# Layer 1's output projection in plain float32 from the weight ring, and seven expert homes taken over at the query products

## The reference

```python
h = rms_norm(x, l1_norm_attn)
x = x + mla_mixer(h, ...)            # ends in: out.reshape(B, S, 1024) @ w_out
h = rms_norm(x, l1_norm_ffn)
logits = h @ w_router                # top 2 of 8 experts, softmax of the two
for e in range(8):
    y = y + combine[..., e:e+1] * swiglu(h, w_gu[e], w_down[e])   # 1024 -> 2 x 3584 -> 1024
x = x + y
```

## Time and profile before

| | us |
|---|---|
| median of 3 runs | 1250.08 |
| lowest and highest run | 1250.06, 1251.47 |
| span of the profiled execution | 1247.9 |
| PE busy | 1208.8 (97%) |
| DVE busy | 530.3 (42%) |
| ACT busy | 336.5 (27%) |
| HBM read | 411.02 MB |

### The profile page before, as it was taken

How to read it: one execution, slowest core, us unless ns; L and a number is a source line. 1 busy time by engine, 2 the same in 40 slices (tenths; PEclk the granted TensorE clock), 3 DMA queues, 4 the chain that set the end, 5 groups by cost and what they waited for, 6 DMA issues and landing times.

```text
span 1247.9 us, 22143 instructions
## 1 busy us (share of the span) xinstructions
PE 1208.8 (97%) x9410; PEld 594.7 (48%) x9410; DVE 530.3 (42%) x1085; ACT 336.5 (27%) x654; POOL 64.0 (5%) x87
## 2 busy tenths in 40 slices
PE   9988999999988999999999999999999999999987
PEld 7767888888777733333433333333333333333321
DVE  6977665555777411331331143243232141413313
ACT  7365555454766300110220011011010012001101
POOL 5300000000530000000000000000000000000000
PEclk9999999999999999999999999999999999999999
DMA  9503545454605999999999999999999999999995
GB/s 345 196 19 138 195 176 187 182 196 121 231 6 223 385 383 418 397 380 417 423 420 423 423 421 422 423 422 406 423 423 421 423 422 421 423 423 420 422 423 233
DMA packets 61001, 413.58 MB, mean 331 GB/s; under 512 B 7120, under 2 KB 7280, under 8 KB 12640
## 3 DMA queue, kind: packets, MB, share of 16 engines
q1 hardware_dynamic: 60048, 411.20, 81.2%
q0 software_dynamic: 560, 0.81, 0.5%
q10 hardware_dynamic: 288, 0.08, 0.0%
HBM read 411.02 MB, written 1.05 MB: 330 GB/s over the span
## 4 chain that ended last, share of the span: by engine, by line
PE 82%; DVE 5%; SPq 4%; DMA 3%; ACT 3%; issue 1%; POOL 1%; DVEq 0%; ACTq 0%; POOLq 0%
PE PS L2465 37%; PE PS L2475 18%; PE PS L1936 6%; PE PS L1938 6%; PE PS L1937 6%; SPq L586 4%; DMA homes<-in_expert_tiles 2%; PE PS L2342 2%; DMA ring<-in_dense_tiles 1%; DVE w_lo L1243 1%; PE PS L2004 1%; PE PS L2049 1%; ACT arena L839 1%; PE PS L2374 1%; PE PS L1957 1%
## 5 line engine op out<-in xcount | busy, mean ns | idle before, releaser
L2465 PE MATMUL PS<-homes,arena 128*32 128x512 f32 x3736 | 409.7, 592 | 3.3 <-DMA homes<-in_expert_tiles 3.3
L2465 PEld LDWEIGHTS PS<-homes,arena 128*32 128x32 f32 x3736 | 120.1, 110 | 282.4 <-issue 270.5
L2475 PE MATMUL PS<-homes,arena 128*32 128x512 f32 x1928 | 213.5, 593 | 4.4 <-DMA homes<-in_expert_tiles 4.4
L1823 DVE SCALAR_TENSOR_TENSOR arena<-arena,PS 64x256 f32<-64x256 f32 x126 | 52.2, 414 | 379.2 <-ACT arena L1179 377.2
L1179 ACT ACTIVATE arena<-PS 64x512 f32<-64x512 f32 x63 | 37.3, 592 | 462.7 <-PE PS L2465 462.7
L1936 PE MATMUL PS<-w_hi,hT_hi 128*128 128x512 f32 (+2 forms) x372 | 141.8, 381 | 5.1 <-DVE w_lo L1243 3.0
L1938 PE MATMUL PS<-w_hi,hT_lo 128*128 128x512 f32 (+2 forms) x372 | 139.3, 374 | 0.0
L1937 PE MATMUL PS<-w_lo,hT_hi 128*128 128x512 f32 (+2 forms) x372 | 139.2, 374 | 0.0
L2475 PEld LDWEIGHTS PS<-homes,arena 128*32 128x32 f32 x1928 | 61.5, 110 | 149.8 <-issue 138.0
L2465 PE MATMUL PS<-arena 128*32 128x512 f32 x928 | 103.2, 592 | 2.2 <-DVE arena L1830 1.7
L1243 DVE TENSOR_TENSOR w_lo<-ring,w_hi 128x1024 fp32r<-128x1024 f32 (+1 forms) x60 | 66.9, 1160 | 32.8 <-ACT w_hi L784 32.6
(11 more groups left out here) (241 smaller groups left out, 1008.3 us busy)
## 6 DMA issues: line engine op xcount, KB each, us to landing
homes<-in_expert_tiles SPq DMA_DIRECT2D x270, 1024.0 KB, 20.2
arena<-in_expert_tiles SPq DMA_DIRECT2D x54, 1024.0 KB, 22.0
ring<-in_dense_tiles SPq DMA_DIRECT2D x49, 1024.0 KB, 4.8
arena<-in_expert_tiles SPq DMA_DIRECT2D x8, 512.0 KB, 7.3
arena<-in_expert_tiles SPq DMA_DIRECT2D x16, 256.0 KB, 7.5
x_res<-in_expert_tiles SPq DMA_DIRECT2D x4, 1024.0 KB, 10.3
ring<-in_dense_tiles SPq DMA_DIRECT2D x6, 512.0 KB, 6.2
ring<-in_dense_tiles SPq DMA_DIRECT2D x2, 832.0 KB, 4.3
```

Source lines behind the costliest of these rows:

```text
L1823: ins = v.scalar_tensor_tensor(out=act_exp[64 * j:64 * (j + 1), g, :], in0=gate[0:64, g, c], scalar=1.0, in1=PS[0:64, gu_banks[k][g], c], ...
L2465: ins = pe.matmul(PS[GROUP * q:GROUP * (q + 1), gu_banks[k][g], :], xT[:, cc, o + g * GROUP:o + (g + 1) * GROUP], quarter(k_home, q), star ...
L2475: ins = pe.matmul(PS[GROUP * q:GROUP * (q + 1), 3 + g, :], tokens_T(k, c, q // 2, g), quarter(k_home, q), start=k == 0 and c == 0, stop=end)
```

## The change

`NSPLIT` is the number of pieces that are still split: all but the four of `OUT1`. Those are multiplied as plain float32, with the ring place as the right operand and a new float32 tile `mT` (8 chunks by 256 tokens) as the left, one matmul in the program for each chunk. `mT` lies in home 12, where `hT_hi` is. In place of the split of the merged halves, DVE copies three of them from PSUM into `mT` and ACT the fourth. The splits of `OUT1` pieces are gone on both engines, inside attention and behind it. A ring place that held an `OUT1` piece is free for an expert piece once the piece is used, where it was free once it was split. The slots of `w_hi` and `w_lo` and home 13 are free once the last query piece that needs them is used. `HOME_OF` follows this: home 14, two ring places, the six slots, home 13, the two early homes, the three late ones, four ring places, home 12, the residual's. The early homes move from positions 8 and 9 of the round to 10 and 11.

```diff
--- before.py
+++ after.py
@@ -222,6 +222,8 @@
 LO_AHEAD = (5, 6)
 U0 = len(STREAM)
 
+NSPLIT = U0 - len(OUT1)
+
 
 
 
@@ -230,15 +232,15 @@
 SLAB_HOMES = 15
 RING_FIRST = 2
 HOME_OF = [14] + [(U0 - RING + i) % RING for i in range(RING_FIRST)]
+for _i in range(SLOTS):
+    HOME_OF += [RING + (NSPLIT - SLOTS + _i) % SLOTS, RING + SLOTS + (NSPLIT - SLOTS + _i) % SLOTS]
+HOME_OF.append(13)
+
+EARLY_HOME = SLAB_HOMES + LATE_HOMES
+HOME_OF += range(EARLY_HOME, EARLY_HOME + len(EARLY))
 HOME_OF += range(SLAB_HOMES, SLAB_HOMES + LATE_HOMES)
 HOME_OF += [(U0 - RING + i) % RING for i in range(RING_FIRST, RING)]
-for _i in range(SLOTS):
-    HOME_OF += [RING + (U0 - SLOTS + _i) % SLOTS, RING + SLOTS + (U0 - SLOTS + _i) % SLOTS]
-HOME_OF += [12, 13]
-
-EARLY_HOME = SLAB_HOMES + LATE_HOMES
-for _i in range(len(EARLY)):
-    HOME_OF.insert(1 + RING_FIRST + LATE_HOMES + 2 + _i, EARLY_HOME + _i)
+HOME_OF.append(12)
 RESIDUAL_HOME = EARLY_HOME + len(EARLY)
 HOME_OF.append(RESIDUAL_HOME)
 assert len(HOME_OF) == PLACES and len(set(HOME_OF)) == PLACES
@@ -353,6 +355,7 @@
         h = sb("h_tok", [P, NT, D])
         hT_hi = placed("hT_hi", [P, KC, SEQ], f32r, 12)
         hT_lo = placed("hT_lo", [P, KC, SEQ], f32r, 13)
+        mT = placed("mT", [P, KC, SEQ], f32, 12)
         aT_hi = placed("aT_hi", [P, 4, SEQ], f32r, 14)
         aT_lo = placed("aT_lo", [P, 4, SEQ], f32r, 14.5)
         ident = sb("ident", [P, P])
@@ -591,6 +594,9 @@
                 n = piece_floats(piece)
                 load(u, A["dense_tiles"][u, :, 0:n], n)
 
+            def last_in_ring(k):
+                return U0 - 1 - (U0 - 1 - k) % RING
+
             def first_free(m):
 
                 k = HOME_OF[m]
@@ -603,10 +609,14 @@
                     sp.wait_ge(pv_done, 32)
                 elif k >= SLAB_HOMES:
                     sp.wait_ge(scored, 16)
+                elif k < RING and last_in_ring(k) < NSPLIT:
+                    sp.wait_ge(lo_ready, 2 * (last_in_ring(k) + 1))
                 elif k < RING:
-                    sp.wait_ge(lo_ready, 2 * (U0 - (U0 - 1 - k) % RING))
+                    sp.wait_ge(used, last_in_ring(k) + 1)
                 elif k < RING + 2 * SLOTS:
-                    sp.wait_ge(used, U0 - (U0 - 1 - (k - RING)) % SLOTS)
+                    sp.wait_ge(used, NSPLIT - (NSPLIT - 1 - (k - RING)) % SLOTS)
+                elif k == 13:
+                    sp.wait_ge(used, NSPLIT)
                 else:
                     sp.wait_ge(used, U0)
 
@@ -789,7 +799,7 @@
             def split_ahead(u):
 
                 v = u + SLOTS
-                if v < U0:
+                if v < NSPLIT:
                     split_piece(v, piece_floats(STREAM[v]))
 
             def after(u, task=None):
@@ -870,12 +880,15 @@
                         exps(j + 2)
                     if j in HI_AHEAD:
                         split_ahead(ahead[HI_AHEAD.index(j)])
-                    if j == 4:
+                    if j == 4 and kind == "AB":
                         split_half(i0, 0, 0, 5)
-                    if j == 5:
+                    if j == 5 and kind == "AB":
                         split_half(i0 + 1, 0, 1, 1)
-                split_half(i0 + 2, 1, 0, 4)
-                split_half(i0 + 3, 1, 1, 5)
+                if kind == "AB":
+                    split_half(i0 + 2, 1, 0, 4)
+                    split_half(i0 + 3, 1, 1, 5)
+                else:
+                    split_bank(i0 + 3, mT[:, 4:8, P:2 * P], bank(5).rearrange("p (c n) -> p c n", c=4))
 
 
             a.dma_start(ident[:, :], A["ident"]).then_inc(ident_loaded, 16)
@@ -1081,9 +1094,6 @@
             transposed_heads(1, 1, range(4))
 
             attention(16, "C", [first(UQ) + i for i in range(len(UQ))], X_MERGE1)
-            for i in range(len(OUT1) - 2):
-                after(first(OUT1) + i)
-
             for g in range(2):
                 a.wait_ge(transposed, X_NORM3 + 2 * g + 1)
                 a.activation(x_cols[:, 4 * g:4 * g + 4, 0:P], bank(g).rearrange("p (c n) -> p c n", c=4), ACT.Copy)\
@@ -1252,7 +1262,7 @@
 
             def split_ahead(u):
                 w = u + SLOTS
-                if w < U0:
+                if w < NSPLIT:
                     split_piece(w, piece_floats(STREAM[w]))
 
             def after(u, task=None):
@@ -1304,7 +1314,14 @@
                 link(v.tensor_scalar(q_scale[:, 0, t, c0:c0 + nh], s, scale, None, ALU.mult))
                 link(v.tensor_scalar(q_scale[:, 1, t, c0:c0 + nh], s, -scale, None, ALU.mult))
 
+            def merged_half(i, t, g, b):
+
+                v.wait_ge(transposed, i + 1)
+                v.tensor_copy(mT[:, 4 * g:4 * g + 4, t * P:(t + 1) * P], bank(b).rearrange("p (c n) -> p c n", c=4))\
+                    .then_inc(lo_split, 1)
+
             def attention(s0, kind, ahead, i0):
+                half_done = split_half if kind == "AB" else merged_half
 
                 def front(i):
 
@@ -1397,17 +1414,18 @@
                     if j + 2 < 8:
                         front(j + 2)
                     if j == 5:
-                        split_half(i0, 0, 0, 5)
+                        half_done(i0, 0, 0, 5)
                     if j == 6:
-                        split_half(i0 + 1, 0, 1, 1)
+                        half_done(i0 + 1, 0, 1, 1)
                     if j in LO_AHEAD:
                         split_ahead(ahead[LO_AHEAD.index(j)])
                     if j % 4 == (2 if kind == "C" else 3):
                         final(j // 4, 0)
                     if j % 4 == 3:
                         final(j // 4, 1)
-                split_half(i0 + 2, 1, 0, 4)
-                split_half(i0 + 3, 1, 1, 5)
+                half_done(i0 + 2, 1, 0, 4)
+                if kind == "AB":
+                    split_half(i0 + 3, 1, 1, 5)
                 split_ahead(ahead[2])
 
             def add_residual(t, n, b):
@@ -1974,6 +1992,13 @@
             def chunk_products(u, t, out, k0, k1):
 
                 c0, w = STREAM[u][2], STREAM[u][4]
+                if u >= NSPLIT:
+                    pe.wait_ge(ring_loaded[u % RING], 16 * (u // RING + 1))
+                    for c in range(k0, k1):
+                        o = (c - c0) * w
+                        ins = pe.matmul(out, mT[:, c, t * P:(t + 1) * P], ring[:, u % RING, o:o + w],
+                                        start=c == 0, stop=c == KC - 1)
+                    return ins
                 s = u % SLOTS
                 for c in range(k0, k1):
                     o = (c - c0) * w
@@ -2134,7 +2159,10 @@
 
                 u0 = first(pieces)
                 for i in range(2):
-                    pe.wait_ge(lo_split, i0 + 3 + i)
+                    if pieces is OUT1 and i == 1:
+                        pe.wait_ge(hi_split, i0 + 1)
+                    else:
+                        pe.wait_ge(lo_split, i0 + 3 + i)
                     piece_products(u0 + i, 1, bank(6)).then_inc(used, 1)
                 piece_products(u0 + 2, 0, bank(1))
                 piece_products(u0 + 2, 1, bank(7)).then_inc(used, 1)
```

## The result

The changed kernel takes 1252.26 us in the median of 20 runs, against 1249.76 for the kernel before in as many. The ratio of the two is 1.0019, with an interval from 1.0013 to 1.0025: it is 2.4 us slower, between 1.6 and 3.1. The forecast was 1253.8, +3.7 on its own base.

A forecast was written before the change was run, and what follows sets the result against it. Weight transfers, waiting for homes that TensorE frees near 850 us, were taken to set the end. Products +5.8, attention -2.1 and homes 0 gave +3.7: span 1251.6, plus 2.2, is 1253.8 us (range 1249.6 to 1257.0).

The forecast's parts named there:

- The products: Output products behind attention: 30 plain float32 products at 0.88 us instead of 0.687, +5.8 us, bounds +5.3 to +7.1.
- the surplus of 0.009: Records of 192 columns take 0.171 us, 0.009 over the scaled 0.162; taken to give 0.441 at 512 columns.
- rival 4: Output products' weight loads: 0.11 us not hidden in each of 60 records, +6.6, 1260.4 us; chance 0.05.
- What leaves attention: Layer 1's attention: without output splits on ACT and DVE, the 22 products start at 396.6, not 398.71: -2.1 us.
- Homes earlier: Expert weight fills: seven more homes filled as the query products end, claimed to gain and cost nothing, 0 us.
- The end follows: Expert transfers wait for homes near 850 us, so the end moves with TensorE's first expert product, +3.7 us.
- Rival 1: Expert transfers: amount loaded sets the end, so earlier homes take 17.4 us off transfers; -5.5, 1244.6 us; chance 0.08.
- rival 2: End of the kernel: TensorE's 9.2 us of waits swallow its 3.7 us delay, 1250.1 us; chance 0.12.
- rival 3: Attention: another wait replaces the splits, so nothing is gained there; +5.8, 1255.9 us; chance 0.07.
- The sum: Whole kernel: span 1247.9 + 3.7 = 1251.6, plus 2.2 from span to median, 1253.8 us, +0.30%.
- the gain of 2.9: Attention: a gain of 2.9 with a product of 0.864 would put the time under 1252.6 us; chance 0.08.
- DVE's later mark: DVE's wait before marking the later slots ends 3.4 us later, covered because its next work comes 6.19 us after.

The follow-up runs named there:

- product-only kernel: Kernel before with only the 32 output products made plain float32; all splits and the fill order stay, ring places held until used: 1257.33 us, ratio 1.0061.
- hold_attention: Changed kernel with its seven early fills held back to the end of layer 1's attention: 1252.31 us, ratio 1.0024.
- ring_held: Kernel before with one SyncE edit: ring places that held an output piece are refilled after its products, not after its split: 1253.08 us, ratio 1.0025.
- old_order: Changed kernel with the order of homes of the kernel before put back: 1255.48 us, ratio 1.0050.
- hold_products: Changed kernel with the split slots' fills, and all 18 fills in the queue, held until the last output product: 1276.15 us, ratio 1.0211.
- half_products: Changed kernel with half of the output products left out (chunks 2 to 5 of the contraction): 1239.17 us, ratio 0.9917.
- attention_alone: Kernel before without the splits of the four output pieces, ring places held until their products: 1250.66 us, ratio 1.0003.

## Why the prediction was right

**The products, +5.8 said, +5.12 measured.** The step stands, and its size was off by 0.7 us. I took 0.44 us a record for the surplus of 0.009 in the row of 192 columns. There is no such surplus at 512 columns: the record is 0.429, and the experts had shown 0.432. The low end of my bounds, +5.3, was the better value. Both weight loads of a product are hidden under the matmul before them, as the group of them in the changed kernel (line, engine, operation, count, busy us, mean ns, idle before) shows: 190 ns each, under records of 429.

```profile
L1999 PEld LDWEIGHTS PS<-ring,mT 128*128 128x128 f32 x60 | 11.2, 190 | 13.4 <-issue 13.4
```

So the rival that rests on the Trainium skill's figure for a weight load ("TensorE: Matmul & The Clock Gate", section "LDWEIGHTS (loading the stationary operand)") fell by the trace. The page's rule gives 107 ns for 128 columns, the trace shows 190, and the measurement decides; but either is a load's length, and on the path stands only what the matmul before it doesn't cover. Two groups of loads in the kernel before agree: the loads of the row of 192 columns last 191 ns, under records that follow each other every 171 ns, and the experts' loads last 110 ns, with records of 432 ns that are no shorter than the 429 here. The 0.11 us that I took for rival 4 is read from no row that I gave. The product-only kernel shows +5.28 at the gather.

**What leaves attention, -2.1 said, -2.50 measured in the trace, of which -2.1 is the change.** The step-by-step chain held: values at 380.51 (said 380.91), at 389.11 (389.5), products at 396.21 (396.6). All three are 0.4 early, and this lead was there before the first split, at the transposes (379.22, and 379.61 before): 0.2 at the first fill, and 0.2 more from 350 to 360 us, where TensorE's granted clock was 0.83 in the kernel before and 1.00 in the changed one. That is a difference between two executions and not the change. The two versions without splits show the second part by themselves. They gain 2.27 and 2.05 at the gather, the first in an execution without this dip (1.00), the second in one with it (0.83), like the kernel before. So 2.05 is the change and 0.2 the dip.

**Homes earlier, 0 said, 0 measured, for a reason that was only half seen.** That early fills bring nothing is shown by hold_attention. What I missed is a cost that the new order avoids. I gave the later freeing of the ring places no price. Plain products hold a ring place until they are done, not until the split. In the old order the two ring places stand ahead of ten other fills, and that wait alone costs 3 us (ring_held, +3.1; old_order, +3.2). That the later fills cost nothing holds in the new order only, where the slots stand first. The new order earns nothing over the old kernel and saves 3 us of what the unsplit products would otherwise cost. A smaller reading was wrong as well: the late homes, said to come some 5 us after 386.48, are issued at 397.77, 11.3 us later, since the queue stands until the end of attention at 394.61. It cost nothing, as hold_attention shows for still later fills.

**The end follows.** The tie to TensorE's place near 850 us held: +2.72 at the first expert product and +2.5 in the span, and -13.76 at the gather and -13.1 in the time with half the products. The rule of the Trainium skill to issue a DMA early ("DMA: Bandwidth & Descriptors", section "Rules for kernel authors") names only the fixed setup cost as what overlaps; I had stretched it to the time of whole transfers. Loading early is worth nothing in the changed kernel, where the homes are full anyway, and 24 us in hold_products, where they are not. Rival 1 and rival 2 fell with hold_attention and half_products, rival 3 with the 396.21, rival 4 with the 0.429.

**The sum.** The change is worth 5.12 - 2.1 = +3.0 us where TensorE stands, and I had 5.8 - 2.1 = +3.7; the miss of 0.7 is the products. In the trace it reads as +2.7, with the 0.4 us of the two executions in it and 0.1 that the row of eight products starts later. The medians say +2.5, between 1.6 and 3.1. The 1253.8 us of the forecast are 1.5 over the measured 1252.26: 0.7 from the products, 0.3 from the base (1250.08 in three runs, 1249.76 in twenty), and about half a microsecond that these runs do not resolve. So the mechanism was right, but the time fell under 1252.6 us, into the part of my forecast to which I had given only 0.08, and not by the gain of 2.9 that I had named for it.

**DVE's later mark** of the slots stayed hidden. The chain names a run of DVE work before the gather of the third expert in the changed kernel, but its place there, 616.41, is 2.72 us behind the kernel before's 613.69, no more than the first expert product. The work behind the mark starts at 606.13 and not 599.98, which is 3.4 us more than that shift, as said, and the 6.19 us of idle time behind it shrink to 2.75.

## What to carry to other kernels

When a stage is bound by transfers into a fixed set of buffers, look for the last time the transfer engines ran thin. If the thin place is made by buffers coming free, earlier loading is worth nothing, as here, and what delays the compute before it comes on the end. That holds only while fills keep up: count the fills behind the compute's start, times the time of one, and compare it with the idle time of the engines before the thin place. Read that idle time from the amount moved in a long window (413 against 421 GB/s here), not from the dip in a short one.

A buffer that is read longer also blocks whatever stands behind it in the queue; ask this of every copy that a change saves. And before taking work out because it delays a critical engine, look where that engine is idle: moving the splits got the same 2 us that leaving them out gives, without the 5 us that the plain products cost.

## What was unexpected of the hardware

Executions of the same program differ by some 4 us with the clock that TensorE is granted. Of 28 runs of the kernel before, taken together, those with a mean granted clock of 0.993 or 0.994 took 1253.05 to 1253.85 us, those at 0.999 took 1248.59 to 1250.16. In the profiled execution of attention_alone the loss stands in layer 0's attention: the window from 60 to 80 us has 0.91 and that from 80 to 100 us 0.92, where the kernel before has 1.00, and its first expert fill comes 2.2 us later. What sets the clock down there in one execution and not in the next stays open, and that it is the clock that makes the 4 us is read from runs that go together, not from a run that sets it. Effects of 2 us were told apart here only by many runs, or by taking places in the trace from a point behind the loss.
